# A conformer convolution with its channel tiles dealt differently between VectorE and TensorE, and a hold on the ring of weight loads

## The reference

```python
def _conformer_conv(h, p):
    z = h @ p["w_pw1"] + p["b_pw1"]
    a, g = jnp.split(z, 2, axis=-1)
    u = a * jax.nn.sigmoid(g)
    u = lax.conv_general_dilated(u, p["w_dw"][:, None, :], window_strides=(1,),
        padding=((CONF_KERNEL // 2, CONF_KERNEL // 2),), dimension_numbers=('NWC', 'WIO', 'NWC'),
        feature_group_count=u.shape[-1]) + p["b_dw"]
    u = jax.nn.silu(_layernorm(u, p["ln_g"], p["ln_b"]))
    return u @ p["w_pw2"] + p["b_pw2"]
```

## Time and profile before

| | |
|---|---|
| profiled execution | 1477.6 us, its span 1475.8 us |
| three timed runs | 1478.33, 1479.55, 1483.22 us |
| PE busy | 1437.4 us, 97% of the span |
| VectorE busy | 1143.3 us, 77% |
| ScalarE busy | 935.1 us, 63% |
| GpSimd busy | 58.1 us, 4% |
| PE clock granted | 0.996 of full speed, mean |
| bytes moved | 478.95 MB, mean 325 GB/s |

### The profile page before, as it was taken

One profiled execution on the slowest core, in us unless ns is written; L12 is line 12 of the kernel. 1 busy time (PEld: TensorE's weight loads), 2 busy tenths in 40 slices (PEclk: granted clock), 3 DMA queues, 4 the chain that ended last, 5 costly groups with the idle time before them and its releaser, 6 DMA issues.

```text
span 1475.8 us, 20341 instructions
## 1 busy us (share of the span) xinstructions
PE 1437.4 (97%) x8408; PEld 1209.7 (82%) x8408; DVE 1143.3 (77%) x1077; ACT 935.1 (63%) x888; POOL 58.1 (4%) x61
## 2 busy tenths in 40 slices
PE   6999999999989999999999999999999999999997
PEld 5778899998968778888888888888888888888885
DVE  3565744445876699889879889878988987988997
ACT  2454643333414677777777777787777777777773
POOL 0210011000011100000000000000000000000010
PEclk9999999999999999999999999999999999999999
DMA  9867776756895499999989999989999998999993
GB/s 374 297 242 271 264 235 228 229 175 217 286 290 209 153 356 373 372 393 373 376 350 375 373 385 377 376 336 388 374 372 395 373 373 352 374 373 388 391 409 132
DMA packets 103571, 478.95 MB, mean 325 GB/s; under 512 B 8556, under 2 KB 39420, under 8 KB 54320
## 3 DMA queue, kind: packets, MB, share of 16 engines
q1 hardware_dynamic: 99696, 465.86, 83.4%
q0 software_dynamic: 3200, 10.98, 2.4%
q10 hardware_dynamic: 576, 0.73, 0.2%
HBM read 471.91 MB, written 5.63 MB: 324 GB/s over the span
## 4 chain that ended last, share of the span: by engine, by line
PE 86%; DVE 6%; DMA 4%; ACT 2%; issue 1%; POOL 0%; ACTq 0%; DVEq 0%; POOLq 0%
PE bank L1731 20%; PE bank L1729 20%; PE bank L1730 20%; PE bank L1735 5%; PE bank L1737 5%; PE bank L1736 5%; DVE low L1594 2%; PE bank L2279 2%; DMA raw<-w_in 1%; PE bank L1772 1%; PE bank L2067 1%; PE bank L2068 1%; PE bank L2069 1%; PE bank L2113 1%; PE bank L1789 1%
## 5 line engine op out<-in xcount | busy, mean ns | idle before, releaser
L1594 DVE TENSOR_TENSOR low<-raw,high 128x2048 fp32r<-128x2048 f32 x333 | 749.7, 2288 | 107.0 <-ACT high L886 105.6
L886 ACT ACTIVATE high<-raw 128x2048 fp32r<-128x2048 f32 x333 | 631.9, 1922 | 103.5 <-DMA raw<-moe 101.5
L1729 PE MATMUL bank<-high,hidH 128*128 128x512 f32 x896 | 349.5, 390 | 0.0
L1731 PE MATMUL bank<-high,hidL 128*128 128x512 f32 x896 | 349.1, 390 | 0.0
L1730 PE MATMUL bank<-low,hidH 128*128 128x512 f32 x896 | 348.6, 389 | 0.0
L1735 PE MATMUL bank<-hidH,high 128*128 128x256 f32 x736 | 211.5, 287 | 3.1 <-DVE hidL L1051 1.3
L1736 PE MATMUL bank<-hidL,high 128*128 128x256 f32 x736 | 208.1, 283 | 0.0
L1737 PE MATMUL bank<-hidH,low 128*128 128x256 f32 x736 | 208.1, 283 | 0.0
L1731 PEld LDWEIGHTS bank<-high,hidL 128*128 128x128 f32 x896 | 168.2, 188 | 35.0
L1729 PEld LDWEIGHTS bank<-high,hidH 128*128 128x128 f32 x896 | 168.2, 188 | 34.7
L1730 PEld LDWEIGHTS bank<-low,hidH 128*128 128x128 f32 x896 | 168.2, 188 | 34.6
(11 more groups left out here) (249 smaller groups left out, 1207.8 us busy)
## 6 DMA issues: line engine op xcount, KB each, us to landing
raw<-moe SPq DMA_DIRECT2D x336, 1024.0 KB, 5.2
raw<-ada_w SPq DMA_DIRECT2D x40, 1024.0 KB, 6.1
raw<-ffn_gu SPq DMA_DIRECT2D x44, 512.0 KB, 5.1
raw<-ffn_down SPq DMA_DIRECT2D x11, 1024.0 KB, 5.4
raw<-ada_first SPq DMA_DIRECT2D x8, 1024.0 KB, 14.9
raw<-w_in SPq DMA_DIRECT2D x8, 1024.0 KB, 8.7
raw<-conv_pw SPq DMA_DIRECT2D x16, 512.0 KB, 5.0
raw<-w_o SPq DMA_DIRECT2D x4, 1024.0 KB, 6.2
```

What stands on the lines that cost most here:

```text
L886: a.activation(high[:, m % SPLITS, :], raw[:, n % RAWS, :], ACT.Copy).then_inc(S("high_ready"), 1)
L1594: v.tensor_tensor(low[:, n % RAWS, :], raw[:, n % RAWS, :], high[:, m % SPLITS, :].bitcast(F32), ALU.subtract).then_inc(S("low_ready"), 1)
L1729: pe.matmul(out, xh, wh, start=start, stop=False)
L1731: return pe.matmul(out, xl, wh, start=False, stop=stop)
```

## The change

VectorE now convolves tiles 0, 1 and 6, and PE tiles 2, 3, 4, 5 and 7. The number of taps on VectorE (93) and of tiles on PE (5) is the same. So unit 1 sends two tiles through DRAM where it sent one, unit 2 sends two as before, and unit 3 sends one where it sent two. The taps are written in another order: tile 6 has its gated rows only after unit 3, and from its fifth tap on its taps stand one behind the other with no second tile between them. On PE the queue is 2, 3, the sum of adaLN group 4, 4, 5, two adaLN pieces, 7. On ScalarE three tiles are brought over before the high part of `pw2 0,0`, one between the two high parts, one behind them. SP waits for `shifted_in3` before it issues `ada 5,2`. What stands behind that load in SP's queue are `ada 5,3`, `5,4`, `5,5`, `pw2 0,0` and everything later.

```diff
-DVE_TILES = 3
-PE_TILES = KT - DVE_TILES
+ON_DVE = (0, 1, 6)
+ON_PE = (2, 3, 4, 5, 7)
...
         def conv_tiles(u):
-            return max(UC * u, DVE_TILES) - DVE_TILES, UC * (u + 1) - DVE_TILES
+            own = [i for i, k in enumerate(ON_PE) if k // UC == u]
+            return own[0], own[-1] + 1
...
             def load(n, piece):
                 slot = n % RAWS
                 arrived = S(f"raw_in{slot}")
+                if piece == ("ada", 5, 2):
+                    sp.wait_ge(S("shifted_in3"), 16 * SHIFTS)
...
             def conv_out(k):
-                a.wait_ge(S("conv_done"), k - DVE_TILES + 1)
+                a.wait_ge(S("conv_done"), ON_PE.index(k) + 1)
...
-            conv_out(DVE_TILES)
-            conv_out(DVE_TILES + 1)
+            conv_out(2)
+            conv_out(3)
+            conv_out(4)
             named("pw2", 0, 0)
-            conv_out(DVE_TILES + 2)
+            conv_out(5)
             named("pw2", 0, 1)
-            conv_out(DVE_TILES + 3)
-            conv_out(KT - 1)
+            conv_out(7)
...
-            conv_taps(0, 9, 1, 9, 6)
-            conv_taps(0, 15, 2, 0, 2)
+            conv_taps(0, 9, 1, 9, 8)
             named("pw1", "b", 3)
             glu(2)
-            conv_taps(0, 17, 2, 2, 13)
+            conv_taps(0, 17, 1, 17, 12)
             glu(3)
-            conv_taps(1, 15, 2, 15, 4)
+            conv_taps(0, 29, 6, 0, 2)
+            conv_taps(1, 29, 6, 2, 2)
+            for j in range(4, 8):
+                conv_tap(6, j)
             rows_out(4)
-            conv_taps(1, 19, 2, 19, 6)
+            for j in range(8, 16):
+                conv_tap(6, j)
             mod_out(4)
-            conv_taps(1, 25, 2, 25, 3)
+            for j in range(16, 26):
+                conv_tap(6, j)
             named("pw2", 0, 0)
-            conv_taps(1, 28, 2, 28, 3)
-            conv_tap(0, 30)
+            for j in range(26, TAPS):
+                conv_tap(6, j)
             named("pw2", 0, 1)
...
+            conv_tile(2)
             conv_tile(3)
+            ada_sum(4)
             conv_tile(4)
-            ada_sum(4)
             conv_tile(5)
             ada_piece(5, 0)
             ada_piece(5, 1)
-            conv_tile(6)
             conv_tile(7)
             ada_piece(5, 2)
             pe.wait_ge(S("conv_part"), DVE_TILES * TAPS)
-            ln_sums(tuple(range(DVE_TILES)), True, False)
-            pe.wait_ge(S("conv_pe_ready"), KT - DVE_TILES)
-            st.mark(ln_sums(tuple(range(DVE_TILES, KT)), False, True), "ln_sum")
+            ln_sums(ON_DVE, True, False)
+            pe.wait_ge(S("conv_pe_ready"), PE_TILES)
+            st.mark(ln_sums(ON_PE, False, True), "ln_sum")
```

More of the change, by code:

```diff
@@ L59 @@
 C_END = C_ID32 + CG
-DVE_TILES = 3
-PE_TILES = KT - DVE_TILES
+ON_DVE = (0, 1, 6)
+ON_PE = (2, 3, 4, 5, 7)
+DVE_TILES = len(ON_DVE)
+PE_TILES = len(ON_PE)
 COLS = {}
@@ L341, in conv_in @@
         def conv_in(k):
-            return uV[:, k] if k < DVE_TILES else uP[:, k - DVE_TILES]
+            return uV[:, ON_DVE.index(k)] if k in ON_DVE else uP[:, ON_PE.index(k)]
         def conv_tiles(u):
-            return max(UC * u, DVE_TILES) - DVE_TILES, UC * (u + 1) - DVE_TILES
+            own = [i for i, k in enumerate(ON_PE) if k // UC == u]
+            return own[0], own[-1] + 1
         def kept_rows(e):
@@ L793, in conv_out @@
             def conv_out(k):
-                a.wait_ge(S("conv_done"), k - DVE_TILES + 1)
+                a.wait_ge(S("conv_done"), ON_PE.index(k) + 1)
                 b = COLS["dw_b"][0] + k
-                st.mark(a.activation(hid[:, k, :], bank[:, 4 + k % 2, 0:TOK], ACT.Identity,
+                st.mark(a.activation(hid[:, k, :], bank[:, 4 + ON_PE.index(k) % 2, 0:TOK], ACT.Identity,
                                      bias=par[:, b:b + 1]), "conv_pe_ready")
@@ L1409, in conv_tap @@
                 dst = hid4[:, k, :, :]
-                src = uV[:, k, :, j:j + P]
-                w = taps[:, j * DVE_TILES + k:j * DVE_TILES + k + 1]
+                src = conv_in(k)[:, :, j:j + P]
+                w = taps[:, j * DVE_TILES + ON_DVE.index(k):j * DVE_TILES + ON_DVE.index(k) + 1]
                 if j == 0:
@@ L2104, in conv_tile @@
             def conv_tile(k):
-                i, u = k - DVE_TILES, k // UC
+                i, u = ON_PE.index(k), k // UC
                 pe.wait_ge(S("taps_spread"), i + 1)
@@ L2113, in conv_tile @@
                         last = pe.matmul(
-                            bank[CG * g:CG * (g + 1), 4 + k % 2, 0:TOK].rearrange("p (t n) -> p t n", t=TILES),
+                            bank[CG * g:CG * (g + 1), 4 + i % 2, 0:TOK].rearrange("p (t n) -> p t n", t=TILES),
                             tapD[:, i, g * ROUNDS + r, :],
@@ L2425, in parameters @@
     dw = np.asarray(inp["conv_dw"][0], dtype=np.float32)
-    put("taps", columns(dw[:, 0:DVE_TILES * P]))
+    put("taps", columns(dw.reshape(TAPS, KT, P)[:, list(ON_DVE)]))
     grouped = np.zeros((SHIFTS * ROUNDS, PE_TILES * P), np.float32)
-    grouped[0:TAPS] = dw[:, DVE_TILES * P:]
+    grouped[0:TAPS] = dw.reshape(TAPS, KT, P)[:, list(ON_PE)].reshape(TAPS, PE_TILES * P)
     grouped = grouped.reshape(ROUNDS, SHIFTS, PE_TILES, GROUPS, CG).transpose(1, 4, 2, 3, 0)
```

## The result

The changed kernel takes 1484.84 us (median of 10 executions, 1484.19 to 1486.83); the kernel before takes 1479.23 (10 executions on the same chip, 1478.02 to 1483.22). The ratio is 1.0042 with an interval of 1.0033 to 1.0051: 5.6 us slower. The profiled execution of after took 1485.59 with a span of 1483.8, against 1477.6 and 1475.8 before.

What follows compares the result with a forecast made beforehand. The prediction took the end of the convolution module, at `ln_sums`, as what counts. A start 4.5 us later plus 1.9 us of clock loss gave +6.4, from 1478.9 to 1485.3 us; range 1481.4 to 1490.4.

Steps and rivals of the forecast that it cites:

- T = 429.0: Landing of the last shifted rows, on which SP waits: forecast at 429.0 us, 9.4 us earlier than the 438.4 of before.
- `pw2 0,0` lands at 443.9: Last of five loads issued together behind SP's wait: lands 14.85 us after the issue, at 443.9, ends 443.0 and 447.4.
- Who waits: ScalarE some 13 us and VectorE some 11 us around `pw2 0,0`; VectorE's last taps later, `ln_sums` starting at 450.85.
- Lone taps 0.51 apart: VectorE's taps of tile 6 with no second tile between: 0.51 us from start to start, where alternating taps take 0.39.
- The clock, +1.9: PE, idle for 10.3 us ahead of `ln_sums`, then runs at half speed at first: 1.9 us lost, ends 0 and 3.65.
- Nothing changes behind `ln_sums`: Everything after the end of `ln_sums` takes as long as before, so its shift is the shift of the whole.
- The sum, +6.4: Whole kernel: `ln_sums` starting 4.5 us later plus 1.9 us of clock loss make it 6.4 us slower.
- The rival of the late rows: Unit 3's shifted rows land up to 6.9 us later than forecast: +8.5 to +13.3 us in all, chance 0.12.
- The rival of the earlier tiles: Not slower, if `pw2 0,0` lands by 439.4 for VectorE's low part; at best 3.3 us faster, 1475.6; chance 0.07.

Runs made afterwards that it cites:

- e6: Changed kernel, hold kept, with the parts of `pw2 0,0` and `pw2 0,1` put behind all tiles and taps, around the squares and the centring: 1475.69 us, ratio 0.9980.
- e7: Changed kernel with 48 spare matmuls on PE ahead of its wait for the taps: 1483.55 us, ratio 1.0034 to the kernel before.
- e2: Kernel before with only SP's wait for `shifted_in3` ahead of `ada 5,2` added, tiles dealt as before: 1488.53 us, ratio 1.0068.
- e5: Changed kernel with SP's wait moved three loads later, from `ada 5,2` to `ada 5,5`: 1482.74 us, ratio 1.0030 to the kernel before.
- e1: Changed kernel without SP's wait for `shifted_in3`, the tiles still dealt anew: 1478.72 us, ratio 1.0002 to the kernel before.
- e8: Changed kernel with `pw2 0,0` and `pw2 0,1` third and fourth in the burst, their parts behind the taps and ScalarE's tiles 5 and 7: 1479.02 us, ratio 1.0006.
- e9: Changed kernel with both ScalarE high parts behind its squares and VectorE's low part of `pw2 0,0` behind the root of the mean: 1476.53 us, ratio 0.9976.
- e10: As e9, but without SP's wait for `shifted_in3`: 1481.07 us, ratio 1.0019 to the kernel before.
- e4: Changed kernel with 40 spare matmuls on PE ahead of its wait for the taps: 1484.90 us, ratio 1.0047 to the kernel before.

## Why the prediction was right

1. *T = 429.0.* Measured 427.86. The write was as forecast (quartet out at 422.73, forecast 422.95). The reads were faster: the last one landed 3.48 us after its issue, where I gave it 4.8, near the 5.0 of the earlier trace rows; that row had stood beside ring loads.
2. *`pw2 0,0` lands at 443.9.* Measured 444.16. Here two errors cancel, which is luck: T was 1.1 earlier, but the burst took 16.3 us from the first issue (427.88), not 14.85. The middle of it moves 420 GB/s as assumed; 5.24 MB in 16.3 − 2.4 us are 377 on average. The Trainium skill's figures from "DMA: Bandwidth & Descriptors", "Anatomy of one DMA — SWDGE (gpsimd) path", 14.0 us by the estimate, are further off; that section gives them for transfers that GpSimd issues, and this burst is issued by SP.
3. *Who waits.* As forecast in order and size: ScalarE 13.13 us (forecast some 13), VectorE 10.90 (some 11), low part from 446.13, five taps, `ln_sums` from 450.96 (forecast 450.85). e6 shows that this order is the cause: with it turned round the same landing holds up nothing ahead of `ln_sums`, and the whole is faster than before.
4. *Lone taps 0.51 apart.* 0.52 in a row of ten (5.23), 0.51 in the last five (2.56), and the chain has them 0.50 long with 0.03 between. The rule of the Trainium skill ("VectorE: DVE Perf Modes", "The DRAIN you can't avoid"), that the next operation doesn't start until the pipe is empty, does not describe the alternating taps: they start 0.39 apart and last 0.48. The section itself adds that an operation that isn't held starts earlier.
5. *The clock, +1.9.* This term was mis-sized: 2.9 by after, 2.8 by e7. I had taken the row nearest in idleness, the sums at the start of the program, and read its 3.68 us as half speed. That reading has no clock row behind it: the granted clock of 11.2 to 14.9 us reads 1.00 in before, and only the length of its matmuls (421 ns, as at a clock of 0.50 in e6, and 275 in the warm sums at 451) speaks for it. And a block of 3.68 us can't show what a longer one loses: here 10.96 us of idleness left `ln_sums` at 0.50 for some 5.8 of its 6.56 us.
6. *Nothing changes behind `ln_sums`.* Right to 0.01 us: 9.62 to pw2's first matmul in before, after, e2 and e5.
7. *The sum, +6.4.* In the profiles +7.5 at L and +8.0 in the span, in the medians +5.6. The forecast of 1485.3 stands 0.5 above the measured 1484.84. By the profiles the sum was 1 us too small, which is the clock; by the medians 0.8 too large. Single executions of these kernels differ by this much, so the medians neither confirm nor refute the last us, and that the forecast stands as near as 0.5 is in part luck: the terms of the burst's start, its length and the clock were each off by 1 to 1.5 us, not all to the same side.

The rival of the late rows did not come. The write of unit 3 was issued 7.8 us behind the second quartet and landed after 2.4 us. What that rival feared is seen without the hold, in e1, where the write came 3.4 us behind the quartet and the last quartet 13.0 behind the write.

The rival of the earlier tiles named the right place, VectorE's low part, and its condition, a landing by 439.4; e8 all but reached it (by 439.57, with the parts behind the taps) and had pw2 begin 3.7 us earlier than before, as that rival would have it. What I had not seen is that the order of ScalarE and VectorE could remove the condition, which is e6 and e9: 1475.69 and 1476.53, faster than both kernels.

What stays open: whether e6 or e9 is the better in time; an order of the loads that brings `pw2 0,0` early without holding its slot for long (e8); and what there would be to gain if e9's low part stayed clear of GpSimd's power and its last adaLN piece came earlier as well.

## What to carry to other kernels

A hold on a shared queue frees the small transfers beside it (6.5 us by e2, 10.5 with the smaller reads), but it turns the loads behind it into a burst, and the price is paid by whoever stands in program order behind the consumer of the burst's last load. Before adding one, list what each engine has queued behind that consumer, and put it in front if it doesn't need the load: the same hold cost 5.9 us in one order (after against e1, by their distances to before) and was worth 4.5 in the other (e10 against e9, by the medians). Look at the loads' order within the burst, too, and at the slots that it takes from the next stage.

## What the runs showed of the hardware

- Small transfers lose more to the ring than I had expected. From a write of 320 KB to the quartet behind it 4.1 us pass with the ring held (after) and 8.6 beside it (e1); with 160 KB 2.7 and 13.0, the latter also behind the reads of another quartet. Reads of 158 KB land in 3.2, where they took 5.0.
- GpSimd's power of 128x2 numbers took 2.77 us beside VectorE's 128x2048 subtraction in e9 and e10 and 0.71 without one beside it in the eleven other kernels. It ends some 0.6 us behind the end of the subtraction in both. The two were not moved against each other by themselves, so this is what thirteen kernels have in common and no more than that.
- TensorE's clock can fall after work has begun again: in e4 PE was idle for 1.84 us ahead of `ln_sums` (from 450.86), and the clock was 1.00 up to 451, 0.68 from 451 to 453 and 0.50 from 453 to 455. In e6 it fell in the same way behind 1.89 us, to 0.50 from 448 to 451. With 0.83 us (e7) it didn't fall, and neither did it behind 2.02 us in e8, where the sum of the squares took its 3.84 us, or through 2.2 us in before. So the length of the last idleness alone doesn't decide it.
